# Routing stage of the expert layers: order of TensorE's products, shape of the mask instructions, place of the first expert's product and of the fourth expert's load

## The reference, cut to what matters

```
g_prob = softmax(t @ w_grp + b_grp)                      # 4 groups
g_w, g_i = top_k(g_prob, 1)
e_logits = (t @ w_rt + b_rt).reshape(n, 4, 8)[n, g_i]    # 8 experts in the chosen group
e_w, e_i = top_k(softmax(e_logits), 2)
weights = e_w / sum(e_w) * g_w
y = sum over the two chosen experts e of weights * (silu(t @ w_gate[e]) * (t @ w_up[e])) @ w_down[e]
```

## Time and profile before

| | us |
|---|---|
| median of 3 runs (lowest, highest) | 1252.37 (1250.38, 1256.89) |
| the profiled execution: its own time | 1246.98 |
| its span in the profile | 1245.2 |
| mean granted clock of TensorE | 0.956 |
| PE busy / DVE / ACT / POOL | 1131.2 / 563.9 / 266.5 / 176.0 |
| DMA | 314.21 MB, mean 252 GB/s |

### The profile page before, as it was taken

The page is one execution under the profiler, slowest core; times in us unless marked ns, Lnnn a source line. Parts: engine busy times, 40 slices in busy tenths (PEclk is TensorE's granted clock), DMA queues, the critical chain, the costliest instruction groups (busy, mean ns, idle before and its releaser), DMA issues.

```text
span 1245.2 us, 26266 instructions
## 1 busy us (share of the span) xinstructions
PE 1131.2 (91%) x9219; PEld 647.4 (52%) x9220; DVE 563.9 (45%) x1222; ACT 266.5 (21%) x648; POOL 176.0 (14%) x261
## 2 busy tenths in 40 slices
PE   6899979989878899999699999999998888999995
PEld 4654656644654455555555654444546544555553
DVE  1031265544443344444633334787555344444445
ACT  2111244440121112212322113221011211221211
POOL 0153120000021111121100001111001111122220
PEclk9999999999788899999899998999996898999998
DMA  9856899740859899999831221000039599987893
GB/s 361 298 191 226 278 331 324 244 147 3 357 226 419 350 415 375 422 422 410 304 113 68 92 78 68 0 1 1 29 106 423 205 421 421 419 348 293 333 421 149
DMA packets 82735, 314.21 MB, mean 252 GB/s; under 512 B 11160, under 2 KB 12097, under 8 KB 57321
## 3 DMA queue, kind: packets, MB, share of 16 engines
q1 hardware_dynamic: 77658, 300.56, 62.1%
q0 software_dynamic: 1952, 6.90, 1.4%
q10 hardware_dynamic: 3056, 5.77, 1.2%
HBM read 307.82 MB, written 5.39 MB: 252 GB/s over the span
## 4 chain that ended last, share of the span: by engine, by line
PE 81%; DVE 5%; DMA 4%; issue 4%; ACT 2%; SPq 2%; POOL 1%; POOLq 0%; ACTq 0%; DVEq 0%
PE banks L472 78%; DMA arena<-in_ada_b 3%; DVE arena L1038 3%; DMA arena<-token_rows,arena 1%; PE banks L669 1%; SPq L1938 1%; PE banks L757 1%; ACT arena L1649 1%; SPq L1936 1%; ACT arena L1659 1%; DVE arena L1188 1%; POOL arena L1842 0%; PE banks L880 0%; PE banks L615 0%; PE banks L523 0%
## 5 line engine op out<-in xcount | busy, mean ns | idle before, releaser
L472 PE MATMUL banks<-arena 32*128 32x256 f32 (+10 forms) x8792 | 1076.0, 414 | 73.1 <-issue 34.2
L472 PEld LDWEIGHTS banks<-arena 128*32 128x32 f32 (+3 forms) x8792 | 595.0, 152 | 530.3 <-issue 402.0
L1038 DVE TENSOR_TENSOR arena<-banks,arena 128x64 f32<-128x64 f32 (+3 forms) x282 | 113.1, 413 | 65.6 <-PE banks L472 59.9
L1038 DVE TENSOR_TENSOR arena<-arena 128x384 f32<-128x384 f32 (+13 forms) x229 | 132.4, 584 | 4.4
L1307 DVE SCALAR_TENSOR_TENSOR arena<-arena 128x768 f32<-128x768 f32 x81 | 84.8, 1047 | 107.5 <-issue 105.2
L1693 ACT ACTIVATE arena<-banks 128x512 f32<-128x512 f32 x79 | 47.2, 597 | 230.6 <-PE banks L472 230.6
L1850 POOL TENSOR_TENSOR arena<-arena 128x256 f32<-128x256 f32 x81 | 59.1, 730 | 229.9 <-PE banks L472 229.9
L1317 DVE TENSOR_SCALAR arena<-arena 128x64 f32<-128x64 f32 x79 | 15.4, 195 | 163.9 <-ACT arena L1697 163.9
L1859 POOL COPY arena<-arena 128x256 f32 x79 | 34.7, 439 | 188.2 <-PE banks L472 148.6
L1829 POOL TENSOR_SCALAR arena<-arena 128x8 f32<-128x8 f32 (+2 forms) x28 | 6.8, 244 | 316.4 <-ACT arena L1540 229.0
L1407 DVE TENSOR_SCALAR arena<-arena 128x385 f32<-128x385 f32 x24 | 11.6, 481 | 82.4 <-ACT arena L1754 82.4
(11 more groups left out here) (152 smaller groups left out, 456.6 us busy)
## 6 DMA issues: line engine op xcount, KB each, us to landing
arena<-in_moe_w_gate SPq DMA_DIRECT2D x64, 1024.0 KB, 8.0
arena<-in_moe_w_up SPq DMA_DIRECT2D x64, 1024.0 KB, 10.3
arena<-in_moe_w_down SPq DMA_DIRECT2D x64, 1024.0 KB, 10.6
arena<-in_ada_w SPq DMA_DIRECT2D x24, 2048.0 KB
arena<-in_hy_w_in SPq DMA_DIRECT2D x6, 2048.0 KB
arena<-in_attn_w_in SPq DMA_DIRECT2D x3, 2048.0 KB
arena<-mod_rows SPq DMA_DIRECT2D x8, 512.0 KB, 9.1
arena<-in_attn_w_out SPq DMA_DIRECT2D x2, 2048.0 KB
```

The source lines that it names most:

```text
L472: return pe.matmul(out, lhsT, rhs, start=start, stop=stop, skip_group_check=True)
L1038: return dve.tensor_tensor(o, p, q, op)
```

## The change

All of it is in the routing stage of both layers, with the start of the expert loop.

- TensorE: the third tile's transposes come before the second tile's logits. The rank product is four matmuls of 96, 64, 32 and 96 columns (before, nine of 32), of which one waits for `count`. `keep_busy(2)` and `keep_busy(3)` are gone. The two weight `rows` products follow `rank`, the two position ones follow `inv`. The slot tiles use banks 2 to 7, and `hidden` of the first expert, with its wait for `moe_x`, stands between the third and the fourth slot tile.
- DVE: each group of three diagonals is one `tensor_tensor` with broadcast operands, those of the weights before the rank is read; the six lane masks are one `tensor_tensor`; `posr` is read behind the two memsets.
- POOL: reads the first expert's bounds right behind the gathers, copies `xcur` as soon as slot tile 0 is in `XS`, then waits for all tiles as before. The first expert's steps are written out, and the loop starts at expert 1.
- SP: the fourth expert's load waits until slot tile 3 has been turned.

```diff
                 transposes(u, (0, 1))
                 logits(0)
+                transposes(u, (2,))
                 logits(1)
-                transposes(u, (2,))
                 close(logits(2), "logit", l)
                 keep_busy(5)
...
-                for t in (2, 1, 0):
-                    for s in range(t + 1):
-                        mm(o[:, t * NE:(t + 1) * NE], upper if s == t else ones, both[:, s, :], s == 0, False)
-                    sig("count").at(pe, l)
-                    last = mm(o[:, t * NE:(t + 1) * NE], cc[0:NE, 0:P], upE, False, True)
-                close(last, "rank", l)
-                keep_busy(2)
+                mm(o[:, 0:3 * NE], upper, both.rearrange("p t e -> p (t e)"), True, False)
+                mm(o[:, NE:3 * NE], ones, both[:, 0:2, :].rearrange("p t e -> p (t e)"), False, False)
+                mm(o[:, 2 * NE:3 * NE], ones, both[:, 0, :], False, False)
+                sig("count").at(pe, l)
+                close(mm(o[:, 0:3 * NE].rearrange("p (t e) -> p t e", t=T), cc[0:NE, 0:P], bc(upE, T, 1), False, True), "rank", l)
...
+                turn_rows(0)
+                turn_rows(1)
                 sig("steps").at(pe, l)
...
-                keep_busy(3)
+                turn_rows(2)
+                turn_rows(3)
...
+                turn_slots((0, 1, 2))
+                pe.wait_ge(gu_loaded[0], 32 + l * 32 * (NE // 4))
+                hidden(0, 0)
+                turn_slots((3, 4, 5))
...
+                for i in range(2):
+                    sig("diag").by(tt(diag[:, 2 + i], bc(ident, T, 1), bc(wt[i], P, 2), ALU.mult), l * 4 + i)
                 slot_of = read(dve, "rank", l)[:, 0:T * NE]
...
-                for c in range(6):
-                    ins = dve.tensor_scalar(lanes[:, c, :], lane, lane_of[:, c:c + 1], None, ALU.is_equal)
-                sig("lo").by(ins, l)
+                sig("lo").by(tt(lanes, bc(lane, 6, 1), bc(lane_of, P, 2), ALU.is_equal), l)
...
-                for r, c in enumerate((pos[:, 6:9], pos[:, 9:12], wt[0], wt[1])):
-                    for t in range(T):
-                        ins = dve.tensor_scalar(diag[:, r, t, :], ident, c[:, t:t + 1], None, ALU.mult)
-                    sig("diag").by(ins, l * 4 + r)
...
+                for i, c in enumerate((pos[:, 6:9], pos[:, 9:12])):
+                    sig("diag").by(tt(diag[:, i], bc(ident, T, 1), bc(c, P, 2), ALU.mult), l * 4 + 2 + i)
...
+                n, b = steps_of(pool, 0)
...
+                sig("xs_a").at(pool, l * ST)
+                sig("xs_d").at(pool, l * ST)
+                pool.wait_ge(s_["moe_pg"], 1)
+                pool.tensor_copy(xcur, XS[:, :, 0:M]).then_inc(s_["moe_x"], 1)
+                sig("xs_a").at(pool, (l + 1) * ST - 1)
+                sig("xs_d").at(pool, (l + 1) * ST - 1)
+                sig("zeroed").at(pool, l)
+                pool.wait_ge(s_["moe_shared"], 1)
+                moved().then_inc(s_["moe_move"], 1)
...
-                with pool.Fori(0, NE) as e:
+                with pool.Fori(1, NE) as e:
...
                 for s in range(4):
+                    if s == 3:
+                        sig("psum_xs").at(sp, (l * ST + 3) * 2 + 1)
                     one(s, s, None)
```

More of the change, by code:

```diff
@@ L724, in moe, with turn_rows @@
                 o = open_(pe, "rank", l, [("pos", l)])
[L725 to L731 removed]
+                mm(o[:, 0:3 * NE], upper, both.rearrange("p t e -> p (t e)"), True, False)
[3 more added lines that the diff above has]
+                close(mm(o[:, 0:3 * NE].rearrange("p (t e) -> p t e", t=T), cc[0:NE, 0:P], bc(upE, T, 1), False, True), "rank", l)
+                def turn_rows(i):
+                    o = open_(pe, "rows", l * 4 + i, [("wr" if i < 2 else "posr", l * 2 + i % 2)])
+                    sig("diag").at(pe, l * 4 + i)
+                    for t in range(T):
+                        last = mm(o[:, t * P:(t + 1) * P], ones, diag[:, (i + 2) % 4, t, :])
+                    close(last, "rows", l * 4 + i)
+                turn_rows(0)
+                turn_rows(1)
                 sig("steps").at(pe, l)
@@ L741, in moe, with turn_slots @@
                 close(last, "inv", l)
[L743 to L746, removed]
-                    for t in range(T):
[L748 to L758, removed]
-                keep_busy(3)
-                first = turn[0] + turn[0] % 2
-                acc = [(("acc", l * 6 + i), [("xffn", l * 3 + (1 if i < 4 else 2))], (first + 2 + i) % 8) for i in range(6)]
-                pg, pt = (open_(pe, n, l, [("moe_end", l)], (first + i) % 8) for i, n in enumerate(("pg", "pt")))
+                turn_rows(2)
+                turn_rows(3)
+                acc = [(("acc", l * 6 + i), [("xffn", l * 3 + (1 if i < 4 else 2))], 2 + i) for i in range(6)]
+                pg, pt = (open_(pe, n, l, [("moe_end", l)], i) for i, n in enumerate(("pg", "pt")))
+                def turn_slots(tiles_):
+                    for i in tiles_:
+                        pe.wait_ge(rows_gathered[i], 16 * (l + 1))
+                        for j in range(2):
+                            n = (l * ST + i) * 2 + j
+                            o = open_(pe, "xs", n, [("xs_a" if j == 0 else "xs_d", l * ST + i)], 2 + (2 * i + j) % 6)
+                            for k in range(4):
+                                c = (4 * j + k) * P
+                                last = pe.transpose(o[:, k * P:(k + 1) * P], slot_rows[:, i, c:c + P], ident)
+                            close(last, "xs", n)
                 py = pt[:, P:P + DE]
@@ L819, in four_experts @@
                     for s in range(4):
-                        pe.wait_ge(gu_loaded[s], (r + 1) * 32 + l * 32 * (NE // 4))
+                        if not (first and s == 0):
+                            pe.wait_ge(gu_loaded[s], (r + 1) * 32 + l * 32 * (NE // 4))
                         if first and s == 0:
-                            hidden(b, s)
                             for k, freed_by, bank in acc:
@@ L1285, in moe @@
                 sig("pos").at(dve, l)
-                for r, c in enumerate((pos[:, 6:9], pos[:, 9:12], wt[0], wt[1])):
-                    for t in range(T):
-                        ins = dve.tensor_scalar(diag[:, r, t, :], ident, c[:, t:t + 1], None, ALU.mult)
-                    sig("diag").by(ins, l * 4 + r)
-                for r in range(2):
-                    sig("posr").by(dve.tensor_scalar(posr[:, r, :], read(dve, "rows", l * 4 + r)[:, 0:NTOK], slot_of_part, None,
-                                                     ALU.subtract), l * 2 + r)
+                for i, c in enumerate((pos[:, 6:9], pos[:, 9:12])):
+                    sig("diag").by(tt(diag[:, i], bc(ident, T, 1), bc(c, P, 2), ALU.mult), l * 4 + 2 + i)
                 dve.memset(yprev, 0.0)
                 link(dve.memset(ysb, 0.0))
+                for r in range(2):
+                    sig("posr").by(dve.tensor_scalar(posr[:, r, :], read(dve, "rows", l * 4 + 2 + r)[:, 0:NTOK], slot_of_part, None,
+                                                     ALU.subtract), l * 2 + r)
                 sig("posr").at(dve, l * 2 + 1)
@@ L1672, in moe @@
                 for r in range(2):
-                    sig("wr").by(act.activation(wr[:, r, :], read(act, "rows", l * 4 + 2 + r)[:, 0:NTOK], ACT.Copy), l * 2 + r)
+                    sig("wr").by(act.activation(wr[:, r, :], read(act, "rows", l * 4 + r)[:, 0:NTOK], ACT.Copy), l * 2 + r)
                 for i in range(ST):
@@ L1850, in moved @@
                     return pool.tensor_tensor(*two, bc(ones, 2), ALU.mult)
-                with pool.Fori(0, NE) as e:
+                sig("xs_a").at(pool, l * ST)
[7 more added lines that the diff above has]
+                moved().then_inc(s_["moe_move"], 1)
+                with pool.If_ne(pool.to_reg(n), 1):
+                    with pool.Fori(1, n) as j:
+                        first = nc.s_assert_within(j * M, 0, SLOTS, skip_runtime_bounds_check_because="a step starts at a slot of its expert")
+                        pool.wait_ge(s_["moe_pg"], b + j + 1)
+                        pool.tensor_copy(xcur, XS[:, :, bass.ds(first, M)]).then_inc(s_["moe_x"], 1)
+                        pool.wait_ge(s_["moe_shared"], b + j + 1)
+                        moved().then_inc(s_["moe_move"], 1)
+                with pool.Fori(1, NE) as e:
                     n, b = steps_of(pool, e)
```

4 lines of the change are left out of this document (1 added, 3 removed).

## The result

The changed kernel took 1245.84 us (median of 10 runs, 1243.03 to 1249.69), the kernel before 1256.4 beside it (10 runs, 1250.38 to 1258.46): ratio 0.9926, 95% interval 0.9904 to 0.9947, so faster by 9.3 us (0.74%). The forecast was 1241.5, or 10.9 us less than the 1252.4 from which it started; the time lies inside the range. The profiled execution took 1243.44 us with a span of 1241.7, only 3.5 less than the span before. The profiled execution of the kernel before, at 1246.98, was faster than all ten timed beside it and 9.4 under their median; the changed kernel's was 2.4 under its own. So the profiles show 7 us less of a gain than the times. Ratios leave out the executions over 1.5% above the fastest of their kernel, which are two: e1's profiled one (1268.14) and one of e5.

What follows compares the result with a forecast made beforehand. PE, busy 91% of the span, was taken as the bound, at half clock in much of routing. Gains of 0.3 + 4.7 + 1.1 + 4.8 = 10.9 us off the 1252.4 median gave 1241.5; range 1233 to 1250.

Steps and rivals of the forecast that it cites:

- step 4: PE through the slot tiles, `hidden` among them: 0.3 us gained in the first layer, 1.1 in the second.
- Step 1: Third tile's transposes before the second tile's logits: +0.5 us per layer, ends -2 and +0.6.
- Step 2: From the choice to the slots: with the logits' reordering, slots 0.2 us earlier, counted as unmoved.
- Step 3: Fourth expert's load held back: gathers land 6.3 us behind their issue, where the first took 8.4.
- The rival with early gathers: Slot tiles: gathers land 2.4 to 4 us behind issue, PE 2.0 sooner in both layers, 1237.5 us; chance 0.20.
- the rival of half clock: Clock stays at half through the slot tiles, losing 4.2 and 3.4 us there: 1250.5 us; chance 0.15.
- Step 5: From the last slot transpose to the second expert step: 4.2 us, gaining 4.7 and 4.8 us.
- The sum's last premise: Expert loops: PE runs step behind step, 5.57 us each, so an earlier second step comes off the end.
- The slower rival: First two rounds of four experts: more half clock, 0.5 us per microsecond, could eat the 10.9; chance 0.10.

Runs made afterwards that it cites:

- e1: The changed kernel, but SP issues the fourth expert's load at once, without the wait for slot tile 3; ratio to the kernel before 0.9987.
- e5: The changed kernel with the five 416-column keep-alive products cut into fifteen of 139 columns in both layers; ratio to the kernel before 0.9919.
- e3: The changed kernel with both tiles' logits again ahead of the third tile's transposes; ratio to the kernel before 0.9924.
- e4: The kernel before with one edit, the fourth expert's load waiting for slot tile 3; ratio to the kernel before 0.9954.
- e9: The kernel before with its five 416-column keep-alive products cut into fifteen of 139 columns, nothing else; ratio to the kernel before 0.9998.
- e6: The changed kernel with keep-alive products cut only in layer 2 and 40 more TensorE instructions in the mixer between the loops; ratio to the kernel before 0.9876.
- e11: e6 with both tiles' logits again ahead of the third tile's transposes; ratio to the kernel before 0.9870.

## Why the prediction was right

Its mechanism held in the routing stages: gathers that land early, and a shorter tail behind the last tile. But one term was much too small (step 4 in the first layer), and two costs behind the routing, of about 7 and 2.7 us, were missing. These partly cancel, so that the total came out near is in part luck. Of the 4.3 us by which the time lies above 1241.5, 4.0 are in the base: the forecast took 10.9 off a median of three runs, 1252.4, and ten runs gave 1256.4.

*Step 1 (+0.5 a layer).* The logits ended 1.8 and 1.4 us later than before; e3 with the old order ended later still. Too small a thing to measure.

*Step 2 (slots unmoved).* Their cast came 0.7 earlier and 0.6 later. DVE's first rank instruction stands directly behind the two diagonals, as forecast, and the six lane masks took 0.95 us. The diagonals and the rank instruction in DVE's timeline, against the earlier trace rows:

```profile
338.94 1.01 DVE L1046 TENSOR_TENSOR arena<-arena 128x384 f32<-128x384 f32 x2
339.88 0.33 DVE L1046 TENSOR_TENSOR arena<-arena,banks 128x192 f32<-128x192 f32 x1
```

*Step 3 (landing 6.3 us).* 4.9 to 5.8 and 4.5 to 6.6. The estimate of 3.2 us, worked out by the formula that the Trainium skill gives in "DMA: Bandwidth & Descriptors", section "Anatomy of one DMA — SWDGE (gpsimd) path", is under all of them: the formula is for one transfer, and here six are issued 1.25 us apart. The rival with early gathers did not come.

*Step 4 (0.3 and 1.1 gained).* The mis-sized term in the first layer: PE was through 3.7 us earlier, for three reasons: slots 0.7 earlier, landing 1.3 sooner than taken, and 8.9 us from the first tile to the last where 10.4 were taken, since the clock stood at full. POOL's copy was in time, ahead of the third tile (its timeline, against the earlier trace rows):

```profile
352.81 0.40 POOL L1861 COPY arena<-arena 128x256 f32<-128x256 f32 x1
```

The second layer had the rival of half clock in part: 0.50 from 955 to 965, 12.3 us in place of 10.4, 0.6 gained where 1.1 was forecast. A low clock at `hidden` was named as a sign of being wrong, and there it was 0.64.

*Step 5 (tail 4.2).* 4.15 and 4.3, so 4.8 gained in each layer where 4.7 and 4.8 were forecast.

*The sum's last premise,* that whatever brings the second step forward comes off the end, failed: "the loops behind them are longer than before" was named as what would show the forecast wrong, and the second is, by 6.2 us. The slower rival had the right place (the first two rounds of four experts) and the right price for the half clock, but left out the stops of 2 to 3 us themselves, and its cause was wrong: not short gaps that moved with the start, but stops that move with the code.

With 13.8 gained in routing, 7 lost by the place of the loops (11 less 4, by the means above) and 2.7 by the bank, 4.1 should be left. The two profiled executions differ by 3.5, and the times by 9.3; where a typical execution of the kernel before loses the 7 us more that its profiled one did not, no profile here shows. A third difference is in no sum here either: from the mixer's first product to the second layer's logits it took 316.5 to 318.3 us in the kernel before, e4 and e9, and 317.1 to 323.1 in the eleven others, seven of them at 322 or more with a granted clock of 0.964 to 0.966 (0.985 in the two at 317). So the mechanism of the gain is shown, and the balance of the whole stays open.

## What to carry to other kernels

While weight loads keep the DMA engines full, the length of the code ahead of a loop can cost or give a few us: compare two versions at equal instruction counts, or try a few paddings, before crediting an edit with that much. Small transfers that the path waits for want the large ones issued behind them (the single most valuable edit here). A total can hide what an edit does: e1's time was that of the kernel before, and its routing stages were 6.3 us shorter. And see how far a profiled execution lies from the median before its stretches are taken for the difference of two times. When work is taken out of a rotation of banks, look at which bank the next stage opens and whose reader it then waits for.

## What was not expected of the hardware

- Forty TensorE instructions more ahead of a loop of unchanged code went with twelve first steps that were 4 us longer in the first loop, and eighty with 11 us shorter ones in the second (means of the groups, one profiled execution of each kernel); the version with the best places found, e6, is at 0.9876 (0.9842 to 0.9910) and e11 at 0.9870 (0.9812 to 0.9927), both below the changed kernel's 0.9926, with intervals that overlap its own.
- With loads of half the size the same twelve steps took 72.0 us in place of 80.4.
- Gathers of 512 KB took 4.3 to 8.0 us where the fourth load was held back and 8.4 to 11.0 where it was not.
